# Hyena's spectrum products written back in PSUM, and the first one-hots ahead of a sum, in a two-layer hybrid encoder

## The reference

```python
def long_conv(u, kf, bias):                    # Hyena, once per order
    uf = jnp.fft.rfft(u, n=2 * L, axis=1)
    y = jnp.fft.irfft(uf * kf[None], n=2 * L, axis=1)[:, :L]   # complex product of two spectra
    return y + u * bias

def hyena_group(...):
    for n, gate in enumerate((x1, x2)):
        z = gate * long_conv(z, kf[:, n], bias[n])

def peer(x, w_query, sub_keys, u_tab, v_tab):
    ...                                        # top 16 of 16 x 16 candidates per head: idx, g
    a = gelu(einsum('thkd,td->thk', u_tab[idx], x))
    return einsum('thk,thkd->td', g * a, v_tab[idx])
```

## Time and profile before

| | |
|---|---|
| timed runs, median of 3 | 1888.85 us |
| the profiled execution's own time | 1890.94 us |
| its span, first to last instruction | 1889.1 us |
| TensorE matmul busy | 1854.6 us, 98% |
| TensorE weight load busy | 1592.4 us, 84% |
| VectorE busy | 1387.3 us, 73% |
| ScalarE busy | 1152.1 us, 61% |
| GpSimd busy | 750.7 us, 40% |
| mean granted TensorE clock | 0.996 |

### The profile page before, as it was taken

One profiled execution on the slowest core, in us unless ns is written; L12 is line 12 of the kernel. 1 busy time (PEld: TensorE's weight loads), 2 busy tenths in 40 slices (PEclk: granted clock), 3 DMA queues, 4 the chain that ended last, 5 costly groups with the idle time before them and its releaser, 6 DMA issues.

```text
span 1889.1 us, 38850 instructions
## 1 busy us (share of the span) xinstructions
PE 1854.6 (98%) x11090; PEld 1592.4 (84%) x11090; DVE 1387.3 (73%) x3018; ACT 1152.1 (61%) x2296; POOL 750.7 (40%) x586
## 2 busy tenths in 40 slices
PE   7999999999999999999999999999999999999998
PEld 6889888888888888878888898888888888888886
DVE  6864998788887666676647659988888866666666
ACT  5744666676765555655566446667666665555554
POOL 6451998576760000010063529876767600000000
PEclk9999999999999999999999999999999999999999
DMA  6335555444445576555542545554444455555554
GB/s 214 101 121 170 174 190 193 147 142 154 140 151 178 191 240 208 189 179 184 192 139 77 156 155 190 180 188 156 144 145 145 145 190 194 194 190 196 191 192 152
DMA packets 90500, 320.04 MB, mean 169 GB/s; under 512 B 10304, under 2 KB 11072, under 8 KB 90176
## 3 DMA queue, kind: packets, MB, share of 16 engines
q1 hardware_dynamic: 90432, 319.20, 51.2%
HBM read 318.11 MB, written 1.05 MB: 169 GB/s over the span
## 4 chain that ended last, share of the span: by engine, by line
PE 92%; DVE 4%; ACT 2%; POOL 1%; issue 1%; DMA 0%; SPq 0%; POOLq 0%; DVEq 0%; ACTq 0%
PE ps L919 25%; PE ps L921 13%; PE ps L992 12%; PE ps L995 12%; PE ps L994 12%; PE ps L941 5%; PE ps L890 2%; PE ps L895 2%; PE ps L892 2%; ACT work L1144 1%; PE ps L906 1%; POOL tab_lo L1429 1%; PE ps L711 1%; PE ps L605 0%; PE ps L800 0%
## 5 line engine op out<-in xcount | busy, mean ns | idle before, releaser
L919 PE MATMUL ps<-x_hl,tab_hi 128*128 128x512 f32 x2048 | 735.3, 402 | 0.0
L1490 POOL TENSOR_TENSOR tab_lo<-raw,tab_hi 128x512 fp32r<-128x512 f32 x448 | 569.3, 1298 | 271.6 <-ACT tab_hi L1270 191.7
L921 PE MATMUL ps<-x_hl,tab_lo 128*128 128x256 f32 x2048 | 572.4, 279 | 0.0
L2069 DVE TENSOR_TENSOR tab_lo<-raw,tab_hi 128x512 fp32r<-128x512 f32 x512 | 356.1, 697 | 256.6 <-ACT tab_hi L1382 255.1
L919 PEld LDWEIGHTS ps<-x_hl,tab_hi 128*128 128x128 f32 x2048 | 384.4, 188 | 86.5
L1270 ACT ACTIVATE tab_hi<-raw 128x512 fp32r<-128x512 f32 x504 | 308.2, 625 | 178.1 <-PE ps L921 177.7
L992 PE MATMUL ps<-tab_lo,w_hi 128*128 128x512 f32 x1024 | 399.5, 390 | 0.7 <-DVE w_lo L2109 0.7
L995 PE MATMUL ps<-tab_hi,w_lo 128*128 128x512 f32 x1024 | 398.5, 389 | 0.0
L994 PE MATMUL ps<-tab_hi,w_hi 128*128 128x512 f32 x1024 | 398.4, 389 | 0.0
L921 PEld LDWEIGHTS ps<-x_hl,tab_lo 128*128 128x128 f32 x2048 | 386.3, 189 | 0.0
L1382 ACT ACTIVATE tab_hi<-raw 128x512 fp32r<-128x512 f32 x512 | 319.8, 625 | 93.1 <-PE ps L995 92.5
(11 more groups left out here) (226 smaller groups left out, 2364.7 us busy)
## 6 DMA issues: line engine op xcount, KB each, us to landing
raw<-tab_u SPq DMA_DIRECT2D x256, 512.0 KB, 3.2
raw<-tab_v SPq DMA_DIRECT2D x256, 512.0 KB, 3.2
raw<-w_proj SPq DMA_DIRECT2D x64, 512.0 KB, 3.6
raw<-w_proj SPq DMA_DIRECT2D x16, 384.0 KB, 3.2
work<-cdft SPq DMA_DIRECT2D x8, 256.0 KB, 5.6
work<-sub_keys SPq DMA_DIRECT2D x2, 1024.0 KB, 4.7
work<-pmat SPq DMA_DIRECT2D x4, 304.0 KB, 5.1
x<-x_in SPq DMA_DIRECT2D x2, 512.0 KB, 4.2
```

What stands on the lines that cost most here:

```text
L919: mm(ps[:, s, :], hi, x_hl[:, 4 * h + k, :, :].rearrange("p a t -> p (a t)"), start=(h + k == 0), stop=False, skip_group_check=True)
L921: last = mm(ps[:, s, 0:256], lo, x_hi[:, 4 * h + k, :], start=False, stop=(h + k == 4), skip_group_check=True)
L1490: tt(half(tab_lo, s, h), half(raw, s, h), half(tab_hi, s, h).bitcast(F32), ALU.subtract).then_inc(lo_pool.sem, 1)
L2069: v.tensor_tensor(half(tab_lo, s, h), half(raw, s, h), half(tab_hi, s, h).bitcast(F32), ALU.subtract).then_inc(lo_dve.sem, 1)
```

## The change

In `hyena_multiply` two of the four products, im Im and re Im, are written back over `im` and `re` in their PSUM banks instead of into `prod`. For this the product im Re, which needs the old `im`, comes second, and a second `link` stands behind it. The difference and the sum then read one operand from SBUF and one from PSUM.

Ahead of the gates, `hot_rows` of groups 0 and 1 and `hot_columns` of group 1 come before the sum of the last plain pair. Inside the first quad they are left out in turn.

```diff
--- before.py
+++ after.py
@@ -1678,11 +1678,11 @@
                     re = ps[:, 1, :].rearrange("p (k c) -> p k c", k=2)
                     im = ps[:, 2, :].rearrange("p (k c) -> p k c", k=2)
                     v.tensor_tensor(prod[:, 0, :, :], re, spec[:, 0:2, o, :], ALU.mult)
-                    v.tensor_tensor(prod[:, 1, :, :], im, spec[:, 2:4, o, :], ALU.mult)
-                    v.tensor_tensor(prod[:, 2, :, :], re, spec[:, 2:4, o, :], ALU.mult)
                     link(v.tensor_tensor(prod[:, 3, :, :], im, spec[:, 0:2, o, :], ALU.mult))
-                    v.tensor_tensor(y_spec[:, 0, :, :], prod[:, 0, :, :], prod[:, 1, :, :], ALU.subtract)
-                    v.tensor_tensor(y_spec[:, 1, :, :], prod[:, 2, :, :], prod[:, 3, :, :], ALU.add)\
+                    v.tensor_tensor(im, im, spec[:, 2:4, o, :], ALU.mult)
+                    link(v.tensor_tensor(re, re, spec[:, 2:4, o, :], ALU.mult))
+                    v.tensor_tensor(y_spec[:, 0, :, :], prod[:, 0, :, :], im, ALU.subtract)
+                    v.tensor_tensor(y_spec[:, 1, :, :], re, prod[:, 3, :, :], ALU.add)\
                         .then_inc(y_spec_done.sem, 1)
 
                 def hyena_gate(o):
@@ -1987,7 +1987,6 @@
                 v.tensor_tensor(w_halves[:, :, 1, 1], rest, w_halves[:, :, 0, 0], ALU.subtract).then_inc(picksT_done.sem, 1)
                 for s in (2, 3):
                     u_lower_early(EARLY // 4 + 1, s)
-                sum_pair(GATE0 // 2 - 1, 2)
                 settled(dve)
 
                 def hot_rows(n, slot):
@@ -2023,12 +2022,13 @@
                         if not (last and s == 3):
                             if not (first and s == 0):
                                 dve.wait_ge(*at(gates_ready, l, n))
-                            hot_rows(n + 1, (s + 1) % 2)
+                            if s or not first:
+                                hot_rows(n + 1, (s + 1) % 2)
                             if s == 2:
                                 sum_pair(i * 2, 0)
                             elif s == 0 and not first:
                                 sum_pair(i * 2 - 1, 2)
-                            if s % 2 == 0:
+                            if s == 2 or s == 0 and not first:
                                 hot_columns(n + 1)
                         if s == 1 and not first:
                             gate_pair(i * 2 - 1, 2, n)
@@ -2042,6 +2042,9 @@
                         weigh_group(n, 4 + s % 2)
 
                 hot_rows(0, 0)
+                hot_rows(1, 1)
+                hot_columns(1)
+                sum_pair(GATE0 // 2 - 1, 2)
                 dve.wait_ge(*at(gelu_done, l, GATE0 // 2))
                 dve.wait_ge(*at(unit_set, l, 3))
                 gate_quad(GATE0 // 4, first=True)
```

## The result

Five timed runs of the changed kernel took 1879.50 to 1880.33 us, 1879.74 at the median; five of the kernel before 1888.13 to 1891.71, 1889.22 at the median. The ratio is 0.9948 (95% interval 0.9934 to 0.9963): 9.5 us faster, where 9.54 us and 1879.3 were forecast. The profiled execution took 1879.74 us (span 1877.9), 11.2 us less than the profiled one before. TensorE's matmul work is busy for 1851.0 us of it.

The account below looks back on a forecast made before the run. TensorE was taken as the bound, busy 1854.6 of 1889.1 us. Products of order 0 (1.60), of order 1 (4.78) and the gate (3.16) sum to 9.54 us, taking the median from 1888.85 to 1879.3, range 1877.2 to 1883.0.

Parts of the forecast that it names:

- Difference and sum at 0.68 us: Hyena products: with one PSUM operand each, L1684 and L1685 no longer wait for GpSimd and take 0.68 us.
- Write-backs cost nothing: Products written back into PSUM: 0 us extra taken, as with L1944; upper bound 1.06 us each.
- The slower rival: Write-backs themselves wait for GpSimd, 1.06 us for each of eight; 1894.6 us, chance 2%.
- No extra for a PSUM source: Difference and sum: the skill's 62 cycles, some 65 ns, for reading PSUM were not expected; they would lose 0.5 us.
- The link's 0.11 us, order 0: Order 0 products: the added link costs 0.11 us; the chain takes 3.90 against 4.70 us, winning 0.80 us per layer.
- Order 1: Order 1 products to the fourth L800: 2.27 us won in layer 0, 2.51 in layer 1, 4.78 together.
- I expect the clock to hold: L711 of order 1: with 0.37 us of idle time left it runs at full clock, 2.05 us against 3.29.
- the prediction's own signs of being wrong: Write-backs over 0.7 us, L711 of order 1 still 3.3 us, or the sum before the gate starting later than before.
- The gates: One-hots done in VectorE's idle time let L941 start 1.58 us earlier per layer, 3.16 us in both.
- tile 2 does not bind: First gate quad: GpSimd's half for tile 2 is ready at 349.87, before TensorE turns to it at 349.96 at the earliest.
- The clock fell in one of two places: Rival: the clock falls in order 1 all the same; 1880.1 us (one layer) or 1880.9 (both), chance 28%.
- the other clock rival: Fall between 963 and 971 goes because the stretch comes 5 us earlier; up to 1.7 us more, 1877.6, chance 7%.

Follow-up runs that it names:

- gpsimd_later: Kernel before, with GpSimd's remainders (L1429) of four tiles held back until VectorE is through with what they met; 1887.14 us, ratio 0.9986.
- one_back: Changed kernel, but only im Im goes back to PSUM, so the sum has two SBUF operands again; 1884.12 us, ratio 0.9975.
- gate_only: Kernel before with the gate's part of the change alone, the products staying in SBUF; 1887.33 us, ratio 0.9989.
- products_only: Changed kernel without the gate's part, so the products' part alone; 1883.76 us, ratio 0.9972.
- group0_only: Changed kernel with only group 0's one-hots ahead of the sum, those of group 1 behind it; 1880.2 us, ratio 0.9953.
- add_later: Changed kernel with VectorE's FNet addition (four L1767) behind Hyena's gate of order 1 instead of ahead of it; 1880.73 us, ratio 0.9951.
- start_held: Changed kernel with 14 filler matmuls alone, in TensorE's idle time at the start of layer 1; 1881.89 us, ratio 0.9958.
- before_wide_sums: Kernel before with the token statistics L784 as matmuls of 128 output columns instead of one, nothing else; 1889.13 us, ratio 0.9992.
- wide_sums_add_later: Changed kernel with 128-column token statistics L784 and the FNet addition behind Hyena's gate of order 1; 1880.68 us, ratio 0.9952.
- wide_sums: Changed kernel with the token statistics L784 as matmuls of 128 equal output columns instead of one; 1879.03 us, ratio 0.9946.

## Why the prediction was right

- **Difference and sum at 0.68 us.** Right in all eight (684 to 689 ns). That the excess was a wait for GpSimd was an inference from rows when the prediction was made; gpsimd_later and one_back show it, the one by taking GpSimd away, the other by leaving one instruction with two SBUF operands. The Trainium skill (SBUF — State Buffer, "Who interferes with whom") says the same: a VectorE instruction with two SBUF inputs contends with a GpSimd one that reads SBUF. The traces agree, and the price here is up to 1.1 us for one instruction.
- **Write-backs cost nothing.** Right: 699 and 689 ns, against 680 to 691 for a multiplication that writes to SBUF. The slower rival (1.06 us each) is refuted.
- **No extra for a PSUM source.** The 62 cycles of the Trainium skill (VectorE: DVE Perf Modes, "The TRN2 errata") would be 65 ns, an estimate by that page. Where GpSimd is silent, difference and sum take 691 and 684 ns (medians) from SBUF alone, and 686 to 689 and 684 with a PSUM operand. The trace does not bear it out for instructions with two operands.
- **The link's 0.11 us, order 0.** Step 0.72 us, gain 0.76 and 0.78 for 0.80.
- **Order 1.** L1685 ends 3.93 us behind L1680's start, forecast 3.90. The new idle time ahead of L800 is 0.67 us in layer 1 (forecast 0.8). What failed is the step "I expect the clock to hold": it held in layer 1 (2.59 us for 2.51) and fell in layer 0 (1.47 for 2.27; 1.59 was the sum for a fall), where L711 takes 3.39 us. That is one of the prediction's own signs of being wrong (3.3 us), and it came in one of two places. The argument was that 1.41 us of idle time ahead of an L711 had not lowered the clock, which took the idle time alone as the cause. The matmuls ahead of the idle time differ too: in order 0 they are L731, 0.38 us each, in order 1 the one-column L784.
- **What lowers the clock.** Over the profiled executions: behind one-column sums with 1.5 us or more of idle time it fell in 6 of 6 places (the kernel before, gate_only, one_back); with 0.28 to 0.44 us in 5 of 12 (changed kernel, products_only, group0_only, add_later, gpsimd_later, start_held); behind wide sums in 0 of 8, two of them with 1.85 us idle. So the one-column sums are part of the cause; for the long idle times two places of one execution show it, and the granted clocks of the 11 runs of before_wide_sums bear them out. For short idle times it is a frequency only, 5 of 12 against 0 of 6: group0_only and products_only are alike there and came out differently.
- **The gates.** 1.58 us each by TensorE's own starts, as forecast. The margin ahead of the sum is 1.43 us for 1.33. That tile 2 does not bind is right: the second and third L941 start at 346.95 and 350.54, without a wait.
- **The rivals.** The clock fell in one of two places, which was priced at 0.8 us. The fall at 963 to 971 went, which was the other clock rival: both happened, in opposite directions. Of the 11 profiled executions without fillers there it fell in 5 (before, gpsimd_later, add_later, wide_sums_add_later, before_wide_sums), at the same idle time of 2.0 us in all. That the stretch comes earlier, the prediction's reason, does not decide it: where L622 starts again at 963.33 and 963.42 (products_only, one_back) the clock held, at 963.63 (gpsimd_later) it fell; at 961.63 and 961.66 (the changed kernel, wide_sums) it held, at 961.76 and 961.30 (add_later, wide_sums_add_later) it fell. So its going is not the change's doing as far as these runs show. The Trainium skill (TensorE: Matmul & The Clock Gate, "What's actually happening") says that the gate's watching runs freely and that transitions vary from run to run. The traces agree with the second, as the same code came out either way; no run here shows the first.

What stays open is what decides, from one execution to the next, whether the clock falls behind a short idle time or at the start of layer 1.

## What to carry to other kernels

When a VectorE instruction takes twice its usual time in some places only, compare its operands with those of its neighbours and see what GpSimd does beside it: one operand in PSUM removes the wait at no cost where the producer can write there. Where the bounding engine waits for such an instruction, work out the gain twice, with its clock held and with its clock fallen, and take the fall as a chance and not as a yes or no: here it came in 5 of 12 places with 0.28 to 0.44 us of idle time. A gain of a few us is to be looked for in the stretches of the traces that were changed, since medians of the same kernel move by 1.4 us. Fillers have to be shorter than the idle time that they fill: count the instructions that a call makes and time one from the trace.

## What the runs showed of the hardware

A VectorE instruction that meets GpSimd on two SBUF operands waits for one GpSimd instruction, the one that runs when it starts, and ends 0.55 us behind it. The rows of GpSimd are from the kernel before (the first two), one_back and gpsimd_later:

```profile
87.61 1.27 POOL L1429 TENSOR_TENSOR tab_lo<-raw,tab_hi 128x512 fp32r<-128x512 f32 x1
104.60 1.72 POOL L1429 TENSOR_TENSOR tab_lo<-raw,tab_hi 128x512 fp32r<-128x512 f32 x1
...
103.59 1.26 POOL L1429 TENSOR_TENSOR tab_lo<-raw,tab_hi 128x512 fp32r<-128x512 f32 x1
...
108.16 1.26 POOL L1429 TENSOR_TENSOR tab_lo<-raw,tab_hi 128x512 fp32r<-128x512 f32 x1
```

They end at 88.88, 106.32, 104.85 and 109.42. The VectorE instructions beside them, L1684 (87.85 + 1.58), L1685 (105.12 + 1.74), L1685 of one_back (103.60 + 1.80) and L1704 (108.47 + 1.50), end at 89.43, 106.86, 105.40 and 109.97, each 0.55 us later. The same holds for all 30 delayed L1684, L1685 and L1704 of the fourteen traces (0.545 to 0.552 us). How long such an instruction takes follows from where in GpSimd's 1.27 us it starts, and that is why the same line takes 0.86 us in one place and 1.80 in another.

GpSimd pays as well, when it starts an instruction while VectorE's is under way: 1.71 to 1.74 us in place of 1.27. In order 1 its four L1429 took 5.88 us beside two waiting instructions, 5.43 beside one (one_back), and 4.98 beside none in the changed kernel. In order 0 before they took 4.97 in spite of one, as it was the last of the four that L1684 waited for the earlier trace rows.

```profile
100.73 4.98 POOL L1429 TENSOR_TENSOR tab_lo<-raw,tab_hi 128x512 fp32r<-128x512 f32 x4 [6.00 <-ACT tab_hi L1038]
```

Narrow outputs save TensorE next to nothing in this chain: with one output column and with 128 alike, all but the first few of the 16 L784 start 0.112 us behind the one before. In no profiled execution did the clock fall behind the wide ones in order 1.
